# Attention of a latent-attention layer: in the first slot of a pair of heads, the products with the values are issued before the turn of the probabilities

## The reference, cut to what matters

```python
for blk in range(S // Q_BLOCK):                      # 8 blocks of 128 queries
    q0, q1 = blk * Q_BLOCK, (blk + 1) * Q_BLOCK
    s = (einsum('bqhd,bkhd->bhqk', q_nope[:, q0:q1], k_nope[:, :q1])
         + einsum('bqhd,bkd->bhqk', q_rope[:, q0:q1], k_rope[:, :q1])) * scale
    s = where(k_chunk[None, :] <= q_chunk[:, None], s, -inf)
    prob = softmax(s, axis=-1)                       # 16 heads
    outs.append(einsum('bhqk,bkhd->bqhd', prob, v[:, :q1]))
```

## Time and profile before

| | us |
|---|---|
| median of 3 runs | 2051.26 (2050.14 to 2051.31) |
| the profiled execution, its own time | 2051.6 |
| its span in the trace | 2049.9 |

### The profile page before, as it was taken

One profiled execution on the slowest core, in us unless ns is written; L12 is line 12 of the kernel. 1 busy time (PEld: TensorE's weight loads), 2 busy tenths in 40 slices (PEclk: granted clock), 3 DMA queues, 4 the chain that ended last, 5 costly groups with the idle time before them and its releaser, 6 DMA issues. The chain is left out here.

```text
span 2049.9 us, 31303 instructions
## 1 busy us (share of the span) xinstructions
PE 1922.3 (94%) x11958; PEld 1361.9 (66%) x11958; DVE 782.4 (38%) x1437; ACT 669.2 (33%) x1486; POOL 614.1 (30%) x658
## 2 busy tenths in 40 slices
PE   7999999999999999999999989999989889798896
PEld 7998878787787777888887767767653233233232
DVE  5224256666553554440112356656521121111114
ACT  5334145555323344331122333333213222222222
POOL 2236387342120110001104576656212122122110
PEclk9999999999999999999999999999999899999988
DMA  7204451211321146523342422121389999999998
GB/s 255 96 32 175 135 195 27 52 27 47 144 72 39 42 80 118 102 54 97 104 103 93 173 82 74 63 73 47 123 348 417 425 425 424 425 424 425 424 424 359
DMA packets 103114, 371.39 MB, mean 181 GB/s; under 512 B 18752, under 2 KB 41664, under 8 KB 76096
## 3 DMA queue, kind: packets, MB, share of 16 engines
q1 hardware_dynamic: 85088, 327.32, 44.3%
q0 software_dynamic: 16704, 42.10, 5.4%
q10 hardware_dynamic: 1184, 0.04, 0.0%
HBM read 325.24 MB, written 60.95 MB: 188 GB/s over the span
## 5 line engine op out<-in xcount | busy, mean ns | idle before, releaser
L2880 PE MATMUL ps<-w_gu,rows_t 128*64 128x512 f32 x1024 | 241.0, 626 | 22.1 <-DMA w_gu<-w_up 20.5
L2880 PEld LDWEIGHTS ps<-w_gu,rows_t 128*64 128x64 f32 x1024 | 74.7, 144 | 163.7 <-issue 140.8
L2899 PE MATMUL ps<-w_d,act_tt 128*64 128x512 f32 x512 | 126.7, 640 | 25.2 <-DMA w_d<-w_down 24.6
L3175 POOL DMA_INDIRECT y_d<-y_out,asg_i x32 | 32.4, 1012 | 368.9 <-DVE y_out L2984 349.4
L2323 PE MATMUL ps<-w_o,mix_t 128*128 128x512 f32 x256 | 123.1, 609 | 0.0
L2975 DVE SCALAR_TENSOR_TENSOR act_g<-ps,rs_c,act_g 128x256 f32<-128x256 f32 x32 | 15.5, 483 | 278.7 <-ACT act_g L2966 278.7
L1110 ACT ACTIVATE prob<-ps,stats 128x1024 f32<-128x1024 f32 (+7 forms) x128 | 94.4, 738 | 62.7 <-DVE stats L1073 62.3
L322 PE MATMUL ps<-tk_lo,h_hi 128*128 128x512 f32 x256 | 99.9, 390 | 0.0
L322 PE MATMUL ps<-tk_hi,h_hi 128*128 128x512 f32 x256 | 99.7, 389 | 0.0
L322 PE MATMUL ps<-tk_hi,h_lo 128*128 128x512 f32 x256 | 99.7, 389 | 0.0
L1073 DVE TENSOR_REDUCE stats<-ps 128x1 f32<-128x1024 f32 (+7 forms) x128 | 97.0, 757 | 4.7 <-DVE ps L1071 0.3
(11 more groups left out here) (481 smaller groups left out, 4429.9 us busy)
## 6 DMA issues: line engine op xcount, KB each, us to landing
w_gu<-w_gate SPq DMA_DIRECT2D x64, 1024.0 KB, 23.5
w_gu<-w_up SPq DMA_DIRECT2D x64, 1024.0 KB, 25.9
w_d<-w_down SPq DMA_DIRECT2D x64, 1024.0 KB, 21.4
w_tk<-w_in SPq DMA_DIRECT2D x5, 2048.0 KB, 17.3
proj_d<-tok_o POOLq DMA_DIRECT2D x40, 256.0 KB, 2.3
tk_in<-proj_d SPq DMA_DIRECT2D x8, 1280.0 KB, 6.0
w_ch<-w_in SPq DMA_DIRECT2D x12, 512.0 KB, 9.1
proj_d<-conv_o POOLq DMA_DIRECT2D x12, 512.0 KB, 4.0
```

The lines of the kernel that those rows point to most:

```text
L2880: mm = pe.matmul(ps[half, 2, :].rearrange("p (g n) -> p g n", g=2), rows_t[:, k, half], w_gu[q][:, h, :, k, :], start=(k == 0), stop=(k == ...
L2899: mm = pe.matmul(ps[half, 4 + j, :], act_tt[:, k, half], w_d[q][:, h, k, j * BANK:(j + 1) * BANK], start=(k == 0), stop=(k == 1))
L3175: pool.indirect_dma_start(out=y_d, out_offset=bass.IndirectOffsetOnAxis(ap=idx, axis=0), in_=y_out[q][:, :], in_offset=None, bounds_check= ...
```

## The change

In the first slot of a pair (j = 0) of pairs 1 to 7, PE issues `values(6)` of the pair before directly behind `scores(0)`, and `turn(14)` behind it. All other slots keep their order, and no other engine is changed. No instruction is added or taken away.

```diff
             def slot(u, p, j, prev):
                 if j < NJ:
                     scores(u, p, j)
-                x = back(u, j, 2, prev)
-                if x and x[1] < NJ:
-                    turn(*x)
                 x = back(u, j, 4, prev)
-                if x and x[1] % 2 == 0:
+                if j == 0 and x:
+                    values(x[0], x[1] // 2)
+                y = back(u, j, 2, prev)
+                if y and y[1] < NJ:
+                    turn(*y)
+                if j > 0 and x and x[1] % 2 == 0:
                     values(x[0], x[1] // 2)
```

## The result

| | us |
|---|---|
| before, median of 6 runs | 2051.31 (2050.14 to 2051.93) |
| changed, median of 6 runs | 2058.85 (2057.29 to 2061.18) |
| ratio | 1.0036, 95% interval 1.0026 to 1.0046 |
| forecast | 2058.4, range 2054.5 to 2060.2 |

The change costs 7.5 us. The interval of the ratio is 5.3 to 9.4 us, so it is slower beyond the 0.2% (4.1 us) that this kernel's measurement can tell.

The account below looks back on a forecast made before the run. PE was taken to set the pace, in the attention and behind it. Seven edges of 1.02 us, 7.1 us on the profiled 2051.6, give 2058.7, or 2058.4 on the median, 0.3 lower; range 2054.5 to 2060.2.

Parts of the forecast that it names:

- The term of an edge: At each of seven edges between pairs, PE's work from `turn(15)` on comes 1.02 us late, between 0.87 and 1.13.
- First step: At the edge, `values(6)` waits on PE for ACT's copy of job 13, so `scores(1)` starts 0.38 us late.
- The bank behind it, second step: `turn(15)` newly waits 0.64 us for DVE's copy of bank 4, so it starts 1.02 us late in all.
- its own sign: A wait of some 0.6 us before `turn(15)`, ended by DVE's copy; without it the time is near 2054.
- Not given back: No later wait of PE, in the pair or behind the attention, takes in the 1.02 us of an edge.
- The wait in slot 5: PE's wait of 0.79 us for DVE's copy descends from `scores(3)`, is late with PE, and so stays.
- Rival one: Only the delay of `scores(1)` at each edge is paid, 7 x 0.38 = 2.7 us, so 2053.9; chance 0.06.
- rival two: The loss is given back in slot 5 of the same pair, 0.23 us staying per edge, so 2052.9; chance 0.05.
- Rival three: Faster: values fill the wait for bank 5 at the edge, `scores(1)` 0.41 us earlier, so 2048.4; chance 0.03.
- the 0.97 us idle in the earlier trace: PE's idle time before a blocked turn in slot 5, read as showing that weight loads aren't pulled across a wait.
- rival four: More than forecast: a further copy becomes late, 0.3 us more for each edge giving 2060.5; chance 0.07.

Follow-up runs that it names:

- before_banks_turned: The kernel before, order unchanged, with the two banks of job 14 exchanged (four tiles to bank 5, the fifth to bank 4); 2055.70 us, ratio 1.0023.
- split_turn: The kernel before, with only the bank 5 tile of `turn(14)` moved behind `values(6)`, the four of bank 4 staying in front; 2050.87 us, ratio 0.9998.
- short_copy: The changed kernel, with DVE copying only one of the four tiles of job 14 out of bank 4 (output not the reference's); 2055.52 us, ratio 1.0020.
- three_edges: The changed kernel, with the new order only at the first three of the seven edges; 2054.92 us, ratio 1.0017.
- out_later_dve: The kernel before, with DVE's copy of the previous pair's outputs moved from slot 3 to slot 4, behind the copy of `turn(2)`; 2050.26 us, ratio 0.9995.
- out_later_both: As out_later_dve, and on ACT in slot 3 the copy of `turn(1)` in front of the copy of the outputs; 2051.30 us, ratio 0.9999.
- after_banks_turned: The changed kernel with the two banks of job 14 exchanged (four tiles to bank 5, the fifth to bank 4); 2057.45 us, ratio 1.0030.
- half_scores_ahead: The changed kernel, with the first of the two banks of `scores(2)` issued in front of `turn(15)` in pairs 1 to 7; 2056.00 us, ratio 1.0022.
- dve_takes_job2: The kernel before, with DVE's copy of the outputs moved to slot 4 and DVE copying both banks of job 2; 2049.73 us, ratio 0.9989.

## Why the prediction was right

**The term of an edge.** Forecast 1.02, measured 1.01 by the ruler. First step: I had the values 0.20 us behind ACT's copy (364.68 to 364.88); they start 0.14 behind (367.70 to 367.84). From there it is 1.03 to `turn(14)` and 0.52 to `scores(1)`, where I had 1.02 and 0.49. On a common clock, from the four tiles of `turn(13)` on, `scores(1)` started 2.67 us later before (363.34 to 366.01) and 3.03 changed (366.36 to 369.39): 0.36 late, forecast 0.38. before_banks_turned loses the cover without the new order (0.49), and split_turn has the values ahead with the cover kept and loses nothing.

**The bank behind it.** The forecast has `turn(15)` start 0.39 + 0.64 = 1.03 us behind `scores(1)`; it is 1.11 at this edge (369.39 to 370.50), so the new delay is 0.72, and 1.01 at the edge before (334.59 to 335.60), so 0.62. The profile's 0.58 and 0.48 are the same delays counted from the modelled end of the last product (369.64 + 0.28 = 369.92 here), 0.14 later than the forecast counts from. The term that was a little off is the way from `turn(14)` to DVE's copy: 0.69 in the forecast, which held at four edges, and 0.79 or 0.80 at three. The whole edge is thus 1.08 here and 0.97 at the edge before, and that the mean comes within 0.01 of the forecast is partly luck; the two steps are not. The forecast named DVE as the engine against what the label came to say. By its own sign, a wait that DVE's copy ends in the profile, its second step would have been called wrong, since the label named ACT; short_copy settled it for DVE. The queue of work that shares a bank was a better guide than the label.

**Not given back.** The wait in slot 5 kept its 0.79, and three_edges shows that no later pair takes the delay in; that no later phase does rests on the medians and on the 954 us behind the attention, so to within some 2 us. Rival one (2053.9) falls with the wait of 0.58, rival two with slot 5. Rival three needed an earlier copy by ACT; PE stood 0.57 us idle for that copy instead. Of rival four, a further copy late, there is no trace in the changed kernel. One reading in the prediction was wrong without weight for the sum: the 0.97 us idle in the earlier trace rows are those of the weight loads, and PE itself sat idle 0.79.

**The size at the end.** 7 x 1.01 = 7.1 stands in the attention; the medians differ by 7.5. The 0.4 lie within the scatter of either kernel's runs (1.8 and 3.9 us from lowest to highest) and stay unexplained.

**Where I was wrong** is in the experiments. Two forecasts were off by most of their size: out_later_dve (a gain of 0.13 for 0.56) and out_later_both (0.03 for 0.54). Both overlooked that the second bank of the same turn waits for ACT. In part off: after_banks_turned (0.29 for 0.36) missed by the start of DVE's copy. Two more were off in part, half_scores_ahead (0.35 for 0.45) and dve_takes_job2 (a further 0.18 for 0.26): they named the next wait at the wrong place, where the next turn of the same bank and DVE's own queue in slot 5 were there to be read in the timeline.

## What to carry to other kernels

Before two neighbours on a queue are exchanged, ask what each of them covers: four transpositions that were ready filled the time of another engine's copy, and the products put in their place waited for that very copy. Then list every use of the shared buffer behind the exchange: with two turns of one bank, the time from the first to the second has to hold turn, copy and both hand-overs (1.53 us at four edges here, 1.63 at three), and an exchange that leaves the amount of work alone can still cut it. A label that names the releaser of a wait for several semaphores is checked by the ends of all of them. And a turn that goes to two banks waits for the later of two copies, so shortening one wait is worth only what the next one leaves.

## What the runs showed of the hardware that I had not expected

The wait before `turn(15)` has two sizes. From the start of `turn(14)` to DVE's copy it is 0.69 us at the edges to pairs 2, 4, 6 and 7 and 0.79 or 0.80 at those to 1, 3 and 5. Two of them, from the timeline of the changed kernel:

```profile
334.07 0.77 PE L988 MATMUL ps<-consts,prob 128*128 128x128 f32 x5
334.76 0.69 DVE L1049 COPY prob_t<-ps 128x512 f32<-128x512 f32 x1 [1.47 <-PE ps L988]
...
334.87 0.28 ACT L1047 ACTIVATE prob_t<-ps 128x128 f32<-128x128 f32 x1 [1.10 <-PE ps L988]
...
438.48 0.76 PE L988 MATMUL ps<-consts,prob 128*128 128x128 f32 x5
439.27 0.69 DVE L1049 COPY prob_t<-ps 128x512 f32<-128x512 f32 x1 [1.56 <-PE ps L988]
439.36 0.28 ACT L1047 ACTIVATE prob_t<-ps 128x128 f32<-128x128 f32 x1 [1.18 <-PE ps L988]
```

At 1, 3 and 5 DVE and ACT begin a turn of their loop (`Fori`, L945), whose body holds an odd pair and the even one behind it; PE's code is written out. ACT's copy of the fifth tile is late there too: 0.88 us behind the turn at the second edge shown against 0.80 at the first. DVE's maximum of slot 0, which stands between the start of the loop's body and the copy, is not: at these two edges it starts 1.43 and 1.44 us behind the start of `turn(13)`. In the kernel before, where the copy doesn't wait for PE but follows that maximum, it starts 0.89 or 0.90 behind the turn at all seven edges. In the changed kernel DVE's copy sets the time, and the 0.10 us show in the distances: 34.78 and 34.89, 34.75 and 34.86, then 34.73 and 34.77, the larger ones those that end at an edge of this kind. So the 0.10 us come with the edges at which the loop turns, but what makes them is open: no run took the loop away.
